# Where the small fp32 blocks stand on TensorE's queue in a one-core hybrid decoder layer: both heads' scores behind unit 7, both groups of value products behind unit 5

## What is computed

```python
h = rmsnorm(x, g_mix_pre)
q_lat, c_kv, k_pe, u_pool, gate_a, gate_p = split_cols(h @ w_in, IN_SIZES)
y_a = mla_branch(q_lat, c_kv, k_pe, positions, ...) @ w_attn_br     # 16 heads, causal softmax
y_p = pool_branch(u_pool, w_pool_grp, pool_scale) @ w_pool_br
x = x + rmsnorm((sigmoid(gate_a) * y_a + sigmoid(gate_p) * y_p) @ w_mix_out, g_mix_post)
h = rmsnorm(x, g_mem_pre)
x = x + rmsnorm(memory_xattn(h, rmsnorm(mem, g_mem_kv), w_mem_q, w_mem_kv, w_mem_o), g_mem_post)
h = rmsnorm(x, g_ffn_pre)
x = x + rmsnorm(conv_gated_ffn(h, w_ffn_in, conv_w, conv_b, w_ffn_out), g_ffn_post)
```

## Time and profile before

| | us |
|---|---|
| median of 3 runs | 1829.41 (1827.87 to 1829.53) |
| the profiled execution | 1829.66 |
| its span, first to last instruction | 1827.9 |
| PE busy | 1810.5 (99%) |
| PE weight loads busy | 1481.5 (81%) |
| DVE busy | 1015.9 (56%) |
| ACT busy | 928.2 (51%) |
| mean granted clock of PE | 0.998 of full speed |

### The profile page before, as it was taken

The page is one execution under the profiler, slowest core; times in us unless marked ns, Lnnn a source line. Parts: engine busy times, 40 slices in busy tenths (PEclk is TensorE's granted clock), DMA queues, the critical chain, the costliest instruction groups (busy, mean ns, idle before and its releaser), DMA issues.

```text
span 1827.9 us, 24021 instructions
## 1 busy us (share of the span) xinstructions
PE 1810.5 (99%) x8228; PEld 1481.5 (81%) x8228; DVE 1015.9 (56%) x1416; ACT 928.2 (51%) x1269; POOL 60.7 (3%) x132
## 2 busy tenths in 40 slices
PE   8999999999999999999999999999999999999998
PEld 7888888888888888888888878888888888888886
DVE  5554455555555554544444476666666666744444
ACT  6555556665546554544444464444444444443443
POOL 4000000000000200000000100000000000000000
PEclk9999999999999999999999999999999999999999
DMA  8455544445556655555434555555555555655553
GB/s 281 150 185 179 172 155 155 155 151 178 188 198 216 207 184 184 169 185 192 144 138 164 192 194 187 184 180 177 177 180 182 183 184 178 234 197 192 189 190 109
DMA packets 166408, 330.69 MB, mean 181 GB/s; under 512 B 7846, under 2 KB 13398, under 8 KB 164950
## 3 DMA queue, kind: packets, MB, share of 16 engines
q1 hardware_dynamic: 164806, 318.48, 52.4%
q10 hardware_dynamic: 1552, 11.54, 1.6%
HBM read 325.81 MB, written 4.19 MB: 181 GB/s over the span
## 4 chain that ended last, share of the span: by engine, by line
PE 96%; ACT 2%; issue 1%; DVE 1%; DMA 0%; SPq 0%; DVEq 0%; ACTq 0%
PE bank L454 30%; PE bank L456 30%; PE bank L455 30%; PE bank L842 1%; PE bank L486 1%; PE bank L770 1%; PE bank L787 1%; DMA bufX<-in_x 0%; PE bank L660 0%; PE bank L669 0%; ACT actA L1233 0%; PE bank L653 0%; PE bank L652 0%; ACT L1087 0%; ACT whi L935 0%
## 5 line engine op out<-in xcount | busy, mean ns | idle before, releaser
L1332 DVE TENSOR_TENSOR wlo<-raw,whi 128x1024 fp32r<-128x1024 f32 x612 | 746.6, 1222 | 757.6 <-ACT whi L935 575.5
L935 ACT ACTIVATE whi<-raw 128x1024 fp32r<-128x1024 f32 x448 | 471.1, 1052 | 604.3 <-PE bank L456 604.2
L454 PE MATMUL bank<-whi,actA 128*128 128x512 f32 x1344 | 542.8, 404 | 2.8 <-DVE actA L1632 1.0
L456 PE MATMUL bank<-whi,actA 128*128 128x512 f32 x1344 | 531.3, 395 | 0.0
L455 PE MATMUL bank<-wlo,actA 128*128 128x512 f32 x1344 | 530.7, 395 | 0.0
L454 PEld LDWEIGHTS bank<-whi,actA 128*128 128x128 f32 x1344 | 253.6, 189 | 60.3 <-issue 2.2
L456 PEld LDWEIGHTS bank<-whi,actA 128*128 128x128 f32 x1344 | 253.2, 188 | 59.3
L455 PEld LDWEIGHTS bank<-wlo,actA 128*128 128x128 f32 x1344 | 253.7, 189 | 55.5
L921 ACT ACTIVATE whi<-raw 128x1024 fp32r<-128x1024 f32 (+1 forms) x164 | 168.9, 1031 | 174.6 <-PE bank L456 170.6
L454 PE MATMUL bank<-whi,actB 128*128 128x512 f32 x576 | 229.4, 398 | 0.0
L456 PE MATMUL bank<-whi,actB 128*128 128x512 f32 x576 | 227.3, 395 | 0.0
(11 more groups left out here) (213 smaller groups left out, 1208.3 us busy)
## 6 DMA issues: line engine op xcount, KB each, us to landing
raw<-in_w_ffn_in SPq DMA_DIRECT2D x88, 1024.0 KB
raw<-in_w_in SPq DMA_DIRECT2D x48, 1024.0 KB
raw<-in_w_mem_kv SPq DMA_DIRECT2D x32, 1024.0 KB
raw<-in_w_ffn_out SPq DMA_DIRECT2D x32, 1024.0 KB
raw<-in_w_attn_br SPq DMA_DIRECT2D x16, 1024.0 KB
raw<-in_w_mix_out SPq DMA_DIRECT2D x16, 1024.0 KB
raw<-in_w_mem_q SPq DMA_DIRECT2D x16, 1024.0 KB
raw<-in_w_mem_o SPq DMA_DIRECT2D x16, 1024.0 KB
```

What stands on the lines that cost most here:

```text
L454: pe.matmul(acc[t][:, 0:n], hi, wh, start=f, stop=False)
L456: mm = pe.matmul(acc[t][:, 0:n], lo, wh, start=False, stop=l)
L935: act.activation(whi[:, ks % AHEAD, 0:w], raw[:, c, ks % 2, 0:w], ACT.Copy).then_inc(hi_done, 1)
L1332: dve.tensor_tensor(wlo[:, vs % AHEAD, 0:w], raw[:, c, vs % 2, 0:w], f32(whi[:, vs % AHEAD, 0:w]), ALU.subtract).then_inc(lo_done, 1)
```

## The change

In the attention loop PE issues the scores of both heads behind unit 7; up to now head 1's came behind unit 8. `s_filled` is still counted up once for each head. In `mem_head` PE issues both groups of value products behind unit 5; up to now the second came behind unit 6. Its own waits for `mpT_out` and `mv_ok` fall away with that, its wait for the bank (`t_wait`) stays. In column 0 of `w_mem_o` the extra call ahead of unit 6 is gone, since step 5 now does both. The lists of ACT, DVE, POOL and SP are not touched.

```diff
-                    if k in (7, 8):
-                        h = k - 7
+                    if k == 7:
                         pe.wait_ge(at_out, f + 3)
-                        for t in range(TT):
-                            w = (t + 1) * P
-                            dst = sc[h][:, t * P:t * P + w]
-                            pe.matmul(dst, qkT[:, h, t * P:(t + 1) * P], qkT[:, h, S:S + w], start=True, stop=False)
-                            mm = pe.matmul(dst, qpeT[:, t * P:(t + 1) * P], kpeT[:, h, 0:w], start=False, stop=True)
-                        mm.then_inc(s_filled, 1)
+                        for h in range(2):
+                            for t in range(TT):
+                                w = (t + 1) * P
+                                dst = sc[h][:, t * P:t * P + w]
+                                pe.matmul(dst, qkT[:, h, t * P:(t + 1) * P], qkT[:, h, S:S + w],
+                                          start=True, stop=False)
+                                mm = pe.matmul(dst, qpeT[:, t * P:(t + 1) * P], kpeT[:, h, 0:w],
+                                               start=False, stop=True)
+                            mm.then_inc(s_filled, 1)
...
-                if k in (5, 6):
+                if k == 5:
                     pe.wait_ge(mpT_out, n + 1)
                     pe.wait_ge(mv_ok, n + 1)
-                    t_wait(T_MOUT + 2 * n + k - 5)
-                    for j in range(2):
-                        d = 2 * (k - 5) + j
-                        for b in range(2):
-                            mm = pe.matmul(tr[(k - 5) % 2][:, j * S:(j + 1) * S], mv_sb[:, b, d * P:(d + 1) * P],
-                                           mpT[:, b, :], start=(b == 0), stop=(b == 1))
-                    mm.then_inc(t_filled, 1)
+                    for g in range(2):
+                        t_wait(T_MOUT + 2 * n + g)
+                        for j in range(2):
+                            d = 2 * g + j
+                            for b in range(2):
+                                mm = pe.matmul(tr[g][:, j * S:(j + 1) * S], mv_sb[:, b, d * P:(d + 1) * P],
+                                               mpT[:, b, :], start=(b == 0), stop=(b == 1))
+                        mm.then_inc(t_filled, 1)
...
         for k in range(8):
-            if k == 6:
-                mem_head(ND - 1)(6)
             if k >= 6:
                 pe.wait_ge(t_out, T_MOUT + k + 1)
             unit(V_MO + k, k, lhs_o, (2 * k, 2 * k + 1), NC, U_MO, k == 0, k == 7)
-            if k != 6:
-                mem_head(ND - 1)(k)
+            mem_head(ND - 1)(k)
```

## The result

| | before | after |
|---|---|---|
| median, us | 1828.93 (4 runs, 1827.87 to 1829.53) | 1839.28 (4 runs, 1839.21 to 1840.73) |
| span of the profiled execution | 1827.9 | 1837.4 |

The ratio is 1.0061, 95% interval 1.0049 to 1.0073: the change makes the kernel slower, by 10.35 us between the two medians (by the ratio it would be 11.2; the executions of before lie up to 1.7 apart). That is only 0.6%, but the interval lies clear of 1. The forecast was 1840.4 with a range of 1838.0 to 1843.0.

What follows compares the result with a forecast made beforehand. TensorE, busy 1810.5 of 1827.9 us, was taken to bound the kernel. Scores +10.5 (8 x 1.31), value products +0.5 and borders 0 made +11.0 us on a median of 1829.41: 1840.4 us, range 1838.0 to 1843.0.

Steps and rivals of the forecast that it cites:

- The stop: PE's wait ahead of head 0's transposes, once a pair: from 0.38 to about 1.7 us, +10.5 us over eight pairs.
- S: PE time of one head's eight score instructions, 1.31 us; the delay of unit 8's end in each pair.
- Both roots: After unit 8, ACT's hi split leads to the exponentials, DVE's lo split to row maximum 1; head 0's normalising needs both.
- a chain of 4.1 to 4.2 us: Work on ACT and DVE from unit 8's end to head 0's transposes, 231.97 to 236.11 in one pair.
- cover of 4.11: PE's work between unit 8's end and head 0's transposes before: head 1's scores 1.31 plus unit 9's 2.80; afterwards 2.80.
- Who is late next: Head 1's transposes after unit 10: normalising ends about 239.7, PE arrives near 240.7, so no second stop.
- The border: Entry and exit cost of a PE block: about 0.01 us, nothing taken for eleven removed; by the skill 1.8 us gain.
- Value products: After the third memory head, the output projection's first matmul waits for DVE's later split: +0.5 us once, bounds 0 and 0.8.
- The upper bound: Sum at most 12.1 us, hence 1841.5: 0.1 more a pair for PE's restart, and 0.8 at the value products.
- Held by head 1's scores: Rival: head 0's normalising waits through row maximum 1 for head 1's scores; stall vanishes, 3.0 us gained, 1826.4; chance 3%.
- No change: Rival: the weights' arrival, not unit 8's end, starts the chain; only 0.5 us left, 1829.9; 5% including an ineffective change.
- The clock: Rival: 1.7 us stops drop PE's clock to 1.2 GHz, 1.7 us each; 1847.2 for half the pairs, 1854.0 for all; 6%.

Runs made afterwards that it cites:

- The scores alone: Kernel before with only the scores moved, both heads' behind unit 7, value products left in two places: 1838.60 us against 1828.24, ratio 1.0059.
- freeing both chains from unit 8: Head 0's exponentials (ACT) and normalising (DVE) put ahead of step 8's weight splits: 1826.38 us on the changed kernel (row maximum 1 also earlier), 1826.34 on the kernel before.
- the kernel without cover: Changed kernel with head 0's transposes of the probabilities behind unit 8 instead of unit 9: 1877.79 us in one run.
- the last experiment on it: Kernel before with the value products part, plus DVE's split of a memory head's second group ahead of its weight split in step 6: 1829.77 us, one run.
- the last kernels of "The cover taken away altogether": Changed kernel with head 0's transposes behind unit 8: 1877.79 us; the same with DVE's row maximum 1 and normalising 0 moved earlier: 1867.58 us; one run each.

## Why the prediction was right

**The stop.** The step that carried the sum was "unit 8 now ends S later, and everything that hangs on its end moves back by S", with S = 1.31. Measured 1.305 a pair, 10.44 in all against 10.5. The scores alone gave +10.4 us, and freeing both chains from unit 8 removed the stop under either order of PE. Both roots that the prediction named, over ACT and over DVE, were shown apart. One working beside it was short: a chain of 4.1 to 4.2 us under a cover of 4.11 would leave a stop of 0.1 at most, not the 0.37 of the rows. The chain was measured from the start of the hi split to the end of the normalising; with the time from unit 8's end to the one and from the other to PE it is 4.47, as the bare stop in the kernel without cover shows. The sum did not use it, since it added S to the measured stop. And the 5.1 us of the earlier trace rows are idle time of the weight load; the stops themselves sum to 2.93.

**Who is late next.** Forecast: head 1's normalising done at 239.7, PE there at 240.7, no second stop. Measured: 238.90 + 0.55 = 239.45 and 240.67, no stop. The 0.2 between the two is mostly that the hi split did not wait for the last read of the exponentials to end (236.59): it starts at 236.49. What the prediction did not see is how thin this slack was once the first stop went away.

**The border.** Taken as nothing. The block of sixteen score instructions costs 230.47 - 227.39 - 0.47 = 2.61, against 2 x 1.31, so the border that is gone was worth nothing that shows. The price of 166 ns for a break, from the Trainium skill (TensorE: Matmul & The Clock Gate, "Single matmul latency"), does not apply at these borders: by it, an estimate, the eight pairs alone would have gained 1.3 us, and the accounts close without.

**Value products.** Forecast +0.5, bounds 0 and 0.8; the trace shows a stop of 0.43 and 0.10 behind it, with the releaser and the place that were named, and the last experiment on it moved the stop away by DVE's order.

**Size.** Forecast +11.0, measured +10.35 by the medians, +10.97 by the traces. The two terms were each right to within 0.1. The upper bound held 0.1 a pair "since a longer stop costs PE a restart"; no run shows such a term: what stands behind a stop is 0.056, and it is the same behind stops of 0.3 and of 1.8 us, so it cancels in the pairs. The difference of the two measures is within the scatter of the runs of before (1827.87 to 1829.53). The level was set a little too high by taking 1829.41 as the median of before; more runs put it at 1828.2 to 1828.9. So the time, 1839.28, came out 1.1 us under the forecast, though the effect was right.

**Rivals.** "Held by head 1's scores" was ruled out by the row maximum's start at 235.46, the end of the lo split. "No change" was ruled out by ACT's idle time of 4.34 us, ended by PE. The clock stayed full at stops of up to 1.84 us; what longer stops do, the last kernels of "The cover taken away altogether" show: they do bring the clock down, so this rival was right in kind and wrong at the length at hand.

## What to carry to other kernels

Moving a block of work on the busiest engine costs nothing by itself; what matters is which of that engine's signals it delays, and how much of the chain behind that signal the rest still covers. Before moving a block, list what hangs on the end of the unit that it is put ahead of, follow the other engines' queues in order, and subtract the cover. And where an engine stands still for a short chain on two in-order engines, look first at what stands ahead of the chain in their queues: here the split of weights wanted four units later stood ahead of a softmax wanted in one, and changing that order was worth 3.4 to 3.7 us, more than the best order of the blocks that was tried (1.7, both heads' scores behind unit 8).

## What the runs showed of the hardware

- Stops of TensorE of up to 1.84 us, among dense matmuls, never lowered its granted clock, in any kernel. Stops of 3.05 us did so once in four times, stops of 4.4 to 4.6 us every time (twelve of twelve), and a fall cost 1.5 to 1.6 us.
- The half clock at the very start comes and goes from one execution to the next: in that of before PE was busy 1.31 of 3.40 us and then ran at half clock, in that of after 2.54 of 3.40 and it did not. It is worth about 1.4 us of span, an eighth of the effect studied here. Of the fourteen traces two show it, that of before and that of the last experiment on the value products; in both PE went 2.45 and 2.55 us from one start to the next just ahead, and in the other twelve 1.3 at most. Those two waits are shorter than the 3.05 us that mostly left the clock up in the loop; they stand among short transposes and not among dense matmuls.
- Float32 blocks and the fp32r units follow each other on TensorE with no cost that these traces can show: a block of eight score instructions costs 1.31 us and one of sixteen 2.61.
- A stop costs PE 0.056 us more than its length ahead of transposes (0.617 against 0.561 us from the first transpose to the second matmul behind), alike for stops of 0.3 and 1.8 us, and 0.10 ahead of a unit (0.34 against 0.24). Eight stops taken away brought 0.45 us beyond their length.
